# Attention's weighted sums in a hybrid decoder trunk: v as the standing operand, probabilities divided on VectorE before they are turned

## The reference

```
def one_block(args):                      # causal attention, 128 queries at a time
    q_blk, blk = args
    sc = jnp.einsum('bhqd,bhkd->bhqk', q_blk, kh) * scale
    ...
    p = jax.nn.softmax(sc, axis=-1)
    return jnp.einsum('bhqk,bhkd->bhqd', p, vh)
...
y = jnp.concatenate([y_mla, o.reshape(b, s, GDN_HEADS * GDN_DV)], axis=-1)
return y @ w_out
```

## Time and profile before

| what | value |
|---|---|
| median of 3 runs | 1062.76 us (1062.66 to 1063.14) |
| the profiled execution's own time | 1061.91 us |
| span of the profiled execution | 1060.0 us |
| PE (TensorE matmul) busy | 1046.9 us, 99% |
| DVE (VectorE) busy | 809.8 us, 76% |
| ACT (ScalarE) busy | 562.6 us, 53% |
| POOL (GpSimd) busy | 46.7 us, 4% |

### The profile page before, as it was taken

The page is one execution under the profiler, slowest core; times in us unless marked ns, Lnnn a source line. Parts: engine busy times, 40 slices in busy tenths (PEclk is TensorE's granted clock), DMA queues, the critical chain, the costliest instruction groups (busy, mean ns, idle before and its releaser), DMA issues.

```text
span 1060.0 us, 19231 instructions
## 1 busy us (share of the span) xinstructions
PE 1046.9 (99%) x8325; PEld 960.7 (91%) x8325; DVE 809.8 (76%) x1072; ACT 562.6 (53%) x695; POOL 46.7 (4%) x32
## 2 busy tenths in 40 slices
PE   9999999999999999999999999999999999999998
PEld 8999987998878999998799999878888889999986
DVE  5887789899854776778987677898666548676797
ACT  6654545685873644445554444555664436444451
POOL 1000000110190000000000000001000000000000
PEclk9999999999999999999999999999999999999999
DMA  9756566463003555565556556566654546555551
GB/s 308 250 187 190 171 199 198 154 202 116 2 5 108 180 192 184 176 198 198 198 163 195 177 182 197 198 201 226 187 164 162 192 155 205 172 187 190 171 196 41
DMA packets 127214, 184.91 MB, mean 174 GB/s; under 512 B 4221, under 2 KB 101738, under 8 KB 127002
## 3 DMA queue, kind: packets, MB, share of 16 engines
q1 hardware_dynamic: 126384, 181.85, 53.1%
q0 software_dynamic: 448, 1.71, 0.5%
q10 hardware_dynamic: 298, 0.12, 0.1%
HBM read 182.62 MB, written 1.05 MB: 173 GB/s over the span
## 4 chain that ended last, share of the span: by engine, by line
PE 80%; DVE 14%; issue 3%; ACT 2%; DMA 1%; SPq 0%; ACTq 0%; DVEq 0%
PE banks L1528 22%; PE banks L1530 22%; PE banks L1529 22%; DVE wlo L968 3%; DVE arena L1040 2%; DVE rounded L1048 2%; PE banks L1689 1%; PE banks L1690 1%; PE banks L1691 1%; DVE arena L1041 1%; DVE raw L1042 1%; PE banks L1981 1%; DVE wlo L1050 1%; PE banks L1606 1%; PE banks L1607 1%
## 5 line engine op out<-in xcount | busy, mean ns | idle before, releaser
L960 DVE TENSOR_TENSOR wlo<-raw,whi 128x2048 fp32r<-128x2048 f32 (+2 forms) x141 | 318.7, 2271 | 101.7 <-ACT whi L500 101.7
L500 ACT ACTIVATE whi<-raw 128x2048 fp32r<-128x2048 f32 (+3 forms) x169 | 309.1, 1841 | 155.9 <-PE banks L1530 138.5
L1528 PE MATMUL banks<-xTh,whi 128*128 128x256 f32 x1360 | 385.3, 283 | 0.2 <-DVE wlo L960 0.2
L1530 PE MATMUL banks<-xTh,wlo 128*128 128x256 f32 x1360 | 384.9, 283 | 0.0
L1529 PE MATMUL banks<-xTl,whi 128*128 128x256 f32 x1360 | 384.9, 283 | 0.0
L1528 PEld LDWEIGHTS banks<-xTh,whi 128*128 128x128 f32 x1360 | 261.1, 192 | 0.4 <-DVE wlo L960 0.4
L1529 PEld LDWEIGHTS banks<-xTl,whi 128*128 128x128 f32 x1360 | 261.1, 192 | 0.0
L1530 PEld LDWEIGHTS banks<-xTh,wlo 128*128 128x128 f32 x1360 | 261.1, 192 | 0.0
L1528 PE MATMUL banks<-whi,hTh 128*128 128x512 f32 (+1 forms) x192 | 77.8, 405 | 1.6 <-DVE wlo L1050 1.6
L1530 PE MATMUL banks<-whi,hTl 128*128 128x512 f32 (+1 forms) x192 | 74.7, 389 | 0.0
L1529 PE MATMUL banks<-wlo,hTh 128*128 128x512 f32 (+1 forms) x192 | 74.5, 388 | 0.0
(11 more groups left out here) (298 smaller groups left out, 1566.0 us busy)
## 6 DMA issues: line engine op xcount, KB each, us to landing
raw<-in_ffn_w_down SPq DMA_DIRECT2D x44, 1024.0 KB, 4.9
raw<-in_ffn_w_gate SPq DMA_DIRECT2D x43, 1024.0 KB, 5.3
raw<-in_ffn_w_up SPq DMA_DIRECT2D x43, 1024.0 KB, 5.4
raw<-in_sg_w_in SPq DMA_DIRECT2D x16, 1024.0 KB, 5.5
raw<-in_ab_w_in SPq DMA_DIRECT2D x8, 1024.0 KB, 5.1
raw<-in_sg_w_out SPq DMA_DIRECT2D x8, 1024.0 KB, 4.8
raw<-in_ab_w_out SPq DMA_DIRECT2D x4, 1024.0 KB, 4.9
raw<-in_ab_w_in SPq DMA_DIRECT2D x2, 832.0 KB, 4.4
```

Of the source, the lines that this page charges most:

```text
L500: A(whi[:, j % SLOTS, 0:n], raw[:, j % RAW_SLOTS, 0:n], ACT.Copy).then_inc(S("hi_ready"), 1)
L960: TT(wlo[:, j % RAW_SLOTS, 0:n], raw[:, j % RAW_SLOTS, 0:n], whi[:, j % SLOTS, 0:n].bitcast(f32), ALU.subtract).then_inc(S("lo_ready"), 1)
L1528: mm(out_ap, lh, rh, start=first, stop=False)
L1530: return mm(out_ap, ll, rh, start=False, stop=last)
```

## The change

The division by the row sums is done before the probabilities are turned. VectorE gets a new function scale_probs: a reciprocal of two columns and two multiplications in place for each head, eight times. The transposes of head h wait for it (probs_scaled) instead of for the exponentials. Of the sums, v now stands in the array and the turned probabilities move: two matrix products for a head where there were three. The result comes with features as rows, heads in pairs, so that the reciprocal and the two multiplications after the last head go, the eight transposes of Y go, and the copies of the high part wait for the sums of the last head (pv_sums). One reduction over squares of the normalised keys (head_sums(1), L1312) moves ahead of the first row maxima.

```
             def yT_hi(k0, k1):
                 for k in range(k0, k1):
-                    act.wait_ge(S("yT_sums"), k // 2 + 1)
+                    act.wait_ge(*((S("pv_sums"), HEADS) if k < 4 else (S("yT_sums"), k // 2 - 1)))
...
+            def scale_probs(h):
+
+                dve.wait_ge(S("exp_done"), 2 * h + 2)
+                link(nc.vector.reciprocal(rden[:, :, h], row_sum[:, :, h]))
+                p = probs[h % 2]
+                TS(p[:, 0, :], p[:, 0, :], rden[:, 0, h:h + 1], None, ALU.mult)
+                TS(p[:, 1:3, :], p[:, 1:3, :], rden[:, 1, h:h + 1], None, ALU.mult).then_inc(S("probs_scaled"), 1)
+
+            head_sums(1)
...
             row_max(0)
             row_max(1)
-            head_sums(1)
+            scale_probs(0)
+            scale_probs(1)
...
-            for n in range(5):
+                    scale_probs(6)
+
+            masked_block(0, 0)
+            scale_probs(7)
+            for n in range(1, 5):
                 masked_block(0, n)
             for n in range(5):
                 masked_block(1, n)
-            dve.wait_ge(S("exp_done"), 2 * HEADS)
-            link(nc.vector.reciprocal(rden, row_sum))
-            dve.wait_ge(S("pv_sums"), HEADS)
-            for t in range(NT):
-                TT(Y[:, t, 0:512].rearrange("p (h d) -> p h d", d=VDIM),
-                   B[t][:].rearrange("p (h d) -> p h d", d=VDIM),
-                   bc(rden[:, t, :].unsqueeze(2), [P, HEADS, VDIM]), ALU.mult).then_inc(S("y_mla"), 1)
...
-                e = slice(VDIM * h, VDIM * h + VDIM)
-                for t, i, tk, a, z in ((0, 0, 0, True, True), (1, 1, 1, True, False), (1, 2, 0, False, True)):
-                    last = mm(B[t][:, e], pT[:, h % 2, P * i:P * i + P], kv_v[:, tk, h, :], start=a, stop=z)
-                last.then_inc(S("pv_sums"), 1)
+                o = B[h // 4][HC[h % 2], 256 * (h // 2 % 2):256 * (h // 2 % 2) + 256]
+                blocks3 = pT[:, h % 2, :].rearrange("p (b n) -> p b n", n=P)
+                mm(o.rearrange("p (b n) -> p b n", n=P), kv_v[:, 0, h, :], blocks3[:, 0:3:2, :], start=True, stop=False,
+                   skip_group_check=True)
+                mm(o[:, P:2 * P], kv_v[:, 1, h, :], blocks3[:, 1, :], start=False, stop=True, skip_group_check=True
+                   ).then_inc(S("pv_sums"), 1)
...
             for h in range(HEADS):
-                pe.wait_ge(S("exp_done"), 2 * h + 2)
+                pe.wait_ge(S("probs_scaled"), h + 1)
...
-            pe.wait_ge(S("y_mla"), 2)
-            y_transposes(0, 4)
```

More of the change, by code:

```diff
@@ L1372, in _ @@
                     row_max(h + 2)
+                if h == 0:
+                    scale_probs(h + 2)
                 if h == 1:
@@ L1378, in _ @@
                                 bc(gcf[:, 8 * t:8 * t + 8].unsqueeze(2), [P, HEADS, 64]), ALU.subtract))
+                    scale_probs(3)
                     TS(Dec, Dec, 0.0, None, ALU.max).then_inc(S("dec_diff"), 1)
@@ L1381, in _ @@
                     head_norm(QKVn[0], 0, float(DK) ** -0.5).then_inc(S("heads_normed"), 1)
+                    scale_probs(4)
                     dve.wait_ge(S("decay_exps"), 2)
@@ L1393, in _ @@
                            ).then_inc(S("decayed"), 1)
+                    scale_probs(5)
                 if h == 4:
```

## The result

The changed kernel takes 1070.85 us (median of 6 runs, 1067.8 to 1072.29) against 1062.8: a ratio of 1.0073, 95% interval 1.006 to 1.0087. It is slower, as forecast, but by 8.1 us and not 5.2, above the range's upper end of 1070.4.

A forecast was written before the change was run, and what follows sets the result against it. VectorE's full list up to the tenth masked block was taken as the bound. 5.4 us ahead of it, -1.2 behind and +1.0 for GpSimd gave +5.2, a median of 1068.0 us, range 1065.4 to 1070.4.

The forecast's parts named there:

- the meeting with GpSimd: At head 7's scaling: its first multiplication waits for GpSimd's first long one, until 295.2, delaying nine masked blocks; +1.0 us.
- the inverse: After yT_lo: the chain stays on TensorE with waits of a few tenths, next to nothing giving time back; 0 us.
- Scalings: VectorE ahead of the tenth masked block: eight scalings, each a reciprocal and two multiplications, 0.74 us each; 5.9 us.
- Waits for exponentials: VectorE must wait for ScalarE's exponentials before scaling heads 0, 1, 2, 4 and 7; together 1.6 us.
- The walk: Following VectorE's and ScalarE's lists head by head with the trace's durations to find VectorE's waits; gave 1.6 us.
- head_sums(1) and the 0.88 wait: Ahead of the tenth masked block: the moved reduction saves 1.2 us, the vanished wait for the last head's scores 0.9.
- GpSimd wins twice: Rival: both of head 7's multiplications wait for GpSimd, until 297.1; +2.9 instead of +1.0, 1069.9 us; chance 0.22.
- Tail: Between tenth masked block and TensorE's return after yT_lo: final reciprocal and two multiplications go, m1 costs 0.26; -1.2 us.
- TensorE's sums: In the heads: the new form takes 0.5 us a head against 0.62, hidden behind TensorE's waits for the scalings.
- TensorE is the bound, and the change is faster: Rival: VectorE has room for the scalings, so only shorter sums and the tail count; 1059.8 us, chance 0.04.

The follow-up runs named there:

- gp_later: Changed kernel, with GpSimd's multiplications after the last head's maxima waiting for head 7's scaling instead; 1066.27 us, ratio to before 1.0033.
- no_division: Changed kernel with the division left out: scale_probs empty, transposes waiting for the exponentials; 1063.45 us, ratio to before 1.001.
- early_scale_old_sums: Changed kernel with VectorE's scalings kept but the old sums and eight transposes of Y back, Y copied from PSUM by VectorE; 1071.56 us, ratio to before 1.0079.

## Why the prediction was right in its mechanism and too small in its sum

The direction, the place (VectorE's full list ahead of the tenth masked block) and the handover at yT_lo were right: TensorE's product behind yT_lo starts at 307.26, 7.4 us later, or 7.65 from S; 5.2 were forecast. Two steps failed above all: the meeting with GpSimd, put at +1.0 us, cost 2.6, and the inverse, put at nothing, cost 1.6. Term by term:

- **Scalings, 5.9 us.** Measured 8 x 0.66 = 5.3. The multiplications were as read the earlier trace rows; the reciprocal of two columns took 0.17 us, the lower bound, not the 0.24 I took from one of 16.
- **Waits for exponentials, 1.6 us.** Measured 0.34, 0.23, 0, 0.99, 0.20, 0, 0 and 0.56, in all 2.3. Head by head right but for head 3, whose wait comes from TensorE at 1.2 GHz. The walk kept TensorE at its high level after a wait that I had myself put at its first transposes. This step failed too. That the sum of the first two terms is nearly right (7.6 against 7.5) is luck: the scalings came out 0.6 shorter and the waits 0.7 longer.
- **head_sums(1) and the 0.88 wait, -2.1 us.** As forecast.
- **The meeting with GpSimd, +1.0 us.** The step that failed most. Both multiplications waited: from 294.43 the second should have begun and the masked blocks 0.27 later, at 294.70; they began at 297.29, +2.6. Taking the meeting away gave 2.9 us of Y - S back. My rival "GpSimd wins twice" named it; I had held one wait likelier because VectorE's instruction had then waited longest. The trace agrees with the Trainium skill here (SBUF — State Buffer, section "Who interferes with whom"): the loser waits for whole instructions, VectorE's two until 0.08 and 0.15 us behind the ends of GpSimd's two.
- **Tail, -1.2 us.** 302.75 to 307.26 is 4.5 against 5.35, -0.8; the second fall of the clock made m1 late (VectorE waits 0.56 us for it before N1). In gp_later, at clock 1.00 there, the same way took 4.17 us, -1.2.
- **TensorE's sums, 0.5 us a head, hidden.** They took 0.80, longer than before. That is hidden in the changed kernel, but it costs 0.8 us once the division is gone. So the rival "TensorE is the bound, and the change is faster" is refuted twice: its sums aren't shorter, and with no scaling at all the kernel isn't faster.
- **The inverse, 0 us.** "Next to nothing there gives time back" looked for a gain only. V - Y is 1.6 us longer, with 2.0 us more of issue gaps. This step failed too: the sum ended where the chain came back to TensorE, as if TensorE's own list took the same time wherever it began. That the gaps have their places by the count of instructions is shown by both kernels with short products. That the eight transposes had kept them short is shown less well: put back for nobody they made V - Y 1.9 us shorter in no_division's trace and the median 0.9 lower; put back with the scalings (early_scale_old_sums) they made V - Y 0.9 shorter, as much as the two traces of the changed kernel differ (30.5 and 31.4). A mended list of before lost its gain in the same place. So the loss of 1.6 us is measured, and its cause, the supply of instructions, is in part argued.

Terms: 5.3 + 2.3 - 2.1 + 2.6 - 0.8 = 7.3 at Y's product (measured 7.65; 0.3 unassigned), and 1.6 in the inverse, 9.3 from S to V. S came 0.25 earlier; the span grew by 9.0, the median by 8.1.

What stays open: how a piece's arrival and the gap 2.3 to 2.8 us behind it hang together, and why moving the borders by 12 or 24 products with their loads moved gaps and no time. The runs show the pulses and the gaps, not the mechanism between them.

## What to carry to other kernels

Before moving work onto an engine, add up its list to the point that others wait for; a division that costs 1.5 us once cost 5.3 us in eight pieces, each with a wait for what it reads. Look which engine begins a long operation at the same moment, and order the two by a semaphore if the trace shows one stretched to the other's end: that one line gave back 2.9 us in the traces and, by the medians, more than half of the loss. Where an engine runs hundreds of very short instructions, a gain ahead of it may be lost in its issue gaps, so read the gaps there before and after, in more than one trace.

## What the runs showed of the hardware

- VectorE multiplications by a column of scalars (fp32, SBUF to SBUF) that met GpSimd multiplications ended only with them: 0.29 and 0.35 us became 1.21 and 2.00, ending 0.08 and 0.15 us after GpSimd's. It came again in the second trace (1.22 and 2.00) and went when GpSimd waited (0.29 and 0.35).
- After waits of TensorE of 1.63 and 3.33 us its granted clock fell to 1.2 GHz for part of the next stretch (means of 0.66 over 5 us and 0.57 over 4 us); unread products in these waits kept it at 2.4 GHz, and in the wait of 1.63 us 24 of 16 columns in bf16 were enough. In one of two traces of the same kernel the shorter wait let it stay up.
- With v standing (64 columns) and fp32 probabilities moving, two passes of 256 columns took 0.57 and two of 128 0.22 us of the chain; six passes with 128 columns standing and 64 moving had taken 0.62.
- While TensorE runs products of 64 columns, a queue of kind "instruction" moves 16 KB every 3.3 to 4.7 us; 127 such products with their loads took 3.1 us. Gaps of 0.2 to 1.3 us stand some 127 products apart or a multiple of it, and 12 or 24 products put in earlier moved them by 12 or 24. Eight unread transposes in a wait made the stretch behind them 1.9 us shorter in one trace of each.
